# Up projections of a gated feed-forward with the product turned: high and low halves of the activations in one matmul

## The reference

```python
D_FF_2 = -(-8 * D_MODEL // (3 * 256)) * 256        # 2816

for l in range(DEPTH):                              # DEPTH = 2
    ...                                             # mixer, then cross attention
    h = rmsnorm(x, norm_ffn[l])                     # x: 256 x 1024
    x = x + (jax.nn.silu(h @ w1[l]) * (h @ w3[l])) @ w2[l]
```

## Time and profile before

| | before |
|---|---|
| median of 3 runs | 1738.66 us (1738.57 to 1738.78) |
| span of the profiled execution | 1736.9 us |
| TensorE busy | 1718.1 us (99%) |
| VectorE busy | 1123.0 us (65%) |
| ScalarE busy | 899.9 us (52%) |
| one steady group of it | 16.82 us |

### The profile page before, as it was taken

How to read it: one execution, slowest core, us unless ns; L and a number is a source line. 1 busy time by engine, 2 the same in 40 slices (tenths; PEclk the granted TensorE clock), 3 DMA queues, 4 the chain that set the end, 5 groups by cost and what they waited for, 6 DMA issues and landing times.

```text
span 1736.9 us, 23278 instructions
## 1 busy us (share of the span) xinstructions
PE 1718.1 (99%) x9541; PEld 1473.2 (85%) x9541; DVE 1123.0 (65%) x1324; ACT 899.9 (52%) x1048; POOL 170.5 (10%) x118
## 2 busy tenths in 40 slices
PE   8999999999999999999999999999999999999998
PEld 7888999888888888999888889888888888988886
DVE  6877655588677765655556686655555768665555
ACT  6665544465575555444455446544445544654443
POOL 2200000025253310000030000000003000000000
PEclk9999999999999999999999999999999999999999
DMA  8436555554535435555564564465546456446552
GB/s 287 172 137 216 185 182 189 194 165 154 189 119 183 162 122 197 192 195 194 170 216 149 204 226 149 131 209 189 180 165 207 157 201 218 146 156 196 193 189 78
DMA packets 160921, 311.10 MB, mean 179 GB/s; under 512 B 5723, under 2 KB 53344, under 8 KB 160048
## 3 DMA queue, kind: packets, MB, share of 16 engines
q1 hardware_dynamic: 158800, 299.33, 51.1%
q0 software_dynamic: 2016, 10.29, 1.7%
HBM read 304.35 MB, written 5.24 MB: 178 GB/s over the span
## 4 chain that ended last, share of the span: by engine, by line
PE 93%; DVE 4%; ACT 1%; issue 1%; DMA 1%; SPq 0%; DVEq 0%; ACTq 0%
PE ps L489 23%; PE ps L491 23%; PE ps L490 23%; PE ps L689 5%; PE ps L690 5%; PE ps L691 5%; PE ps L449 4%; DVE wlo L1549 1%; PE ps L623 1%; PE ps L647 1%; ACT whi L1001 1%; DVE nat L2086 1%; DMA raw<-in_a_w_qkv 1%; DVE hT_lo L1575 0%; DVE wide L2078 0%
## 5 line engine op out<-in xcount | busy, mean ns | idle before, releaser
L1549 DVE TENSOR_TENSOR wlo<-raw,whi 128x2048 fp32r<-128x2048 f32 x278 | 638.0, 2299 | 390.5 <-ACT whi L1001 390.1
L489 PE MATMUL ps<-whi,hT_hi 128*128 128x512 f32 (+1 forms) x1872 | 736.0, 393 | 3.0 <-DVE hT_lo L1575 0.8
L491 PE MATMUL ps<-whi,hT_lo 128*128 128x512 f32 (+1 forms) x1872 | 726.6, 388 | 0.0
L490 PE MATMUL ps<-wlo,hT_hi 128*128 128x512 f32 (+1 forms) x1872 | 725.7, 388 | 0.0
L1001 ACT ACTIVATE whi<-raw 128x2048 fp32r<-128x2048 f32 x278 | 531.8, 1914 | 349.6 <-PE ps L491 297.6
L489 PEld LDWEIGHTS ps<-whi,hT_hi 128*128 128x128 f32 x1872 | 351.8, 188 | 76.2 <-issue 6.6
L491 PEld LDWEIGHTS ps<-whi,hT_lo 128*128 128x128 f32 x1872 | 351.5, 188 | 73.1
L490 PEld LDWEIGHTS ps<-wlo,hT_hi 128*128 128x128 f32 x1872 | 352.0, 188 | 67.8
L689 PE MATMUL ps<-hT_hi,whi 128*128 128x256 f32 x768 | 218.7, 285 | 0.2
L691 PE MATMUL ps<-hT_hi,wlo 128*128 128x256 f32 x768 | 217.2, 283 | 0.0
L690 PE MATMUL ps<-hT_lo,whi 128*128 128x256 f32 x768 | 217.2, 283 | 0.0
(11 more groups left out here) (234 smaller groups left out, 1168.1 us busy)
## 6 DMA issues: line engine op xcount, KB each, us to landing
raw<-in_w_in SPq DMA_DIRECT2D x46, 1024.0 KB, 5.1
raw<-in_w SPq DMA_DIRECT2D x88, 512.0 KB, 4.5
raw<-in_m_w_up SPq DMA_DIRECT2D x32, 1024.0 KB, 5.2
raw<-in_m_w_down SPq DMA_DIRECT2D x32, 1024.0 KB, 4.9
raw<-in_kv_w SPq DMA_DIRECT2D x24, 1024.0 KB, 5.1
raw<-in_w SPq DMA_DIRECT2D x22, 1024.0 KB, 4.9
raw<-in_b_w_q SPq DMA_DIRECT2D x12, 1024.0 KB, 5.1
raw<-in_a_w_qkv SPq DMA_DIRECT2D x11, 1024.0 KB, 5.9
```

The source lines that it names most:

```text
L489: pe.matmul(acc, xh, wh, start=start and k == 0, stop=False)
L490: pe.matmul(acc, xh, wl, start=False, stop=False)
L491: ins = pe.matmul(acc, xl, wh, start=False, stop=stop and k == kc - 1)
L1549: vec.tensor_tensor(wlo[:, m % SPLIT, :], raw[:, m % RAW, :], whi[:, m % SPLIT, :], ALU.subtract).then_inc(*mark("lo_ready", ("lo", m)))
```

## The change

Only the up groups of the second block's feed-forward, and what follows them, are changed.

- The high and the low half of `hT[i]` become two halves of one buffer, `hT_both[i]`, so that one matmul can take a row block of both: 2 x 256 columns.
- `up_apart` takes the place of `chunk`. The weights are stationary, 128 columns at a time (4 blocks a tile: two of `w1`, two of `w3`), each block with a bank of its own. For each weight block and row block there is one matmul of 512 columns, `whi` by high and low tokens side by side, and one of 256, `wlo` by high tokens, added onto the first half of the bank. That is 2 x 4 x 4 x 2 = 64 matmuls a group. Four banks are used in place of two: `ACC`, `ACC + 1` and `OB`, `OB + 1` in group 0, `ACC`, `ACC + 1` and `TB`, `TB + 1` later.
- The product now has the tokens along the free axis, so r is needed as a row. VectorE writes r 128 times side by side (`r_wide`, L2227 of the changed kernel), TensorE turns that with two transposes after up group 0 (L999), ScalarE copies the row out (L1527).
- For each pair of banks ScalarE copies the low products out (L1533), VectorE adds them to the high ones (L2234) and multiplies by r (L2235). ScalarE makes the sigmoid (L1535), VectorE two products (L2237, L2238). ScalarE rounds the result into the high half of `hT[1]` (L1538), VectorE makes the low half (L2241). All of these are on 512 columns, as 2 x 256 where two banks are read.
- The gated chunk is not turned any more: `ff_turn`, its four transposes, and the copies L1018 and L1568 of it are gone. The down tile waits for `ff lo`.
- On VectorE the split that stood behind the gating of group 0 now stands ahead of it.

```diff
@@ TensorE
+            def up_apart(banks, turned=None, early=None):
+                ch = c.ch
+                hi, both = hT[0][0], hT_both[0]
+                for k0 in (0, 4):
+                    m = c.m
+                    pe.wait_ge(*at("lo", m))
+                    for nb in range(4):
+                        if k0 == 0 and (nb % 2 == 0 or early is not None and nb < 2):
+                            pe.wait_ge(*at("acc free", ch - 1, nb if early is not None and nb < 2 else nb // 2))
+                        for k in range(4):
...
+                            pe.matmul(ps[:, banks[nb], :], wh, both[:, :, k0 + k, :], start=k0 == k == 0, stop=False)
+                            ins = pe.matmul(ps[:, banks[nb], 0:S], wl, hi[:, k0 + k, :], start=False, stop=k0 == 4 and k == 3)
+                        if nb % 2:
+                            ins.then_inc(*mark("products", ("acc", m, nb // 2, 0)))
+                        if early is not None and k0 == 0 and nb == 1:
+                            early()
...
-                chunk(hT[0], tx[v + 2], early=lambda: x_half(v + 2, 1))
...
+                up_apart(UP_FIRST, tx[v + 2], lambda: x_half(v + 2, 1))
+                pe.wait_ge(*at("r wide", l))
+                for t in range(T):
+                    ins = pe.transpose(ps[:, SC, t * P:(t + 1) * P], r_wide[:, t, :], ident[:])
+                ins.then_inc(*mark("row_turned", ("r turned", l)))
                 for j in range(1, NG + 1):
                     if j < NG:
-                        chunk(hT[0], early=ff_turn if j == 1 else None)
-                    k0 = 2 * ((j - 1) % 2)
+                        up_apart(UP_LATER)
+                    pe.wait_ge(*at("ff lo", l, j - 1))
                     final = j == NG and l == L2 - 1
-                    tile(hT[1], k0, DN, j == 1, j == NG, tu[j - 1] - k0 // 2, None,
-                         ff_turn if j < NG else None if final else lambda: x_half(v + 3, 0), None, final)
+                    tile(hT[1], 2 * ((j - 1) % 2), DN, j == 1, j == NG, None, None,
+                         None if j < NG or final else lambda: x_half(v + 3, 0), None, final)
```

More of the change, by code:

```diff
@@ L702, in up_chunk @@
                         slot(n + k0 // 4)
+            def up_apart(banks, turned=None, early=None):
[8 more added lines that the diff above has]
+                        for k in range(4):
+                            if turned is not None and nb == 0 and k % 2 == 0:
+                                pe.wait_ge(*at("T free", turned + (k0 + k) // 2))
+                            w = k * 512 + nb * P
+                            wh, wl = whi[:, m % SPLIT, w:w + P], wlo[:, m % SPLIT, w:w + P]
+                            pe.matmul(ps[:, banks[nb], :], wh, both[:, :, k0 + k, :], start=k0 == k == 0, stop=False)
[4 more added lines that the diff above has]
+                            early()
+                    c.m += 1
+                c.ch += 1
             def mlp(v):
@@ L1500, in _ @@
                             begin(v + 2, junk2)
[L1501 to L1502 removed]
                         tick()
                         m = c.m - 1
[L1505 to L1511 removed]
+                        if j == 0:
+                            act.wait_ge(*at("r turned", l))
+                            sc.activation(r_row, ps[:, SC, 0:S], CP).then_inc(*mark("row_scales_turned", ("r row", l)))
+                        for b in range(2):
+                            act.wait_ge(*at("acc", m, b, 0))
+                            if j:
+                                act.wait_ge(*at("acc free", c.ch - 1, b))
+                            first = (UP_LATER if j else UP_FIRST)[2 * b]
+                            sc.activation(f_low[b], ps[:, first:first + 2, S:2 * S], CP).then_inc(*mark("low_products", ("ff low", l, j, b)))
+                        act.wait_ge(*at("ff scaled", l, j))
+                        sc.activation(f_s, f_a, ACT.Sigmoid).then_inc(*mark("sigmoids", ("fsig", l, j)))
+                        act.wait_ge(*at("ff", l, j))
+                        k = 2 * (j % 2)
+                        sc.activation(hT[1][0][:, k:k + 2, :], f_u, CP).then_inc(*mark("ff_hi", ("ff hi", l, j)))
                         c.ch += 1
@@ L2200, in _ @@
                             begin(v + 2)
[L2201 to L2204, removed]
+                            dve.wait_ge(*at("rs", v + 2))
+                            vec.tensor_copy(r_wide, bc(rst[:, o:o + T], 2, P)).then_inc(*mark("row_scales_wide", ("r wide", l)))
+                        tick()
                         if j == 0:
[L2206 to L2216, removed]
+                            dve.wait_ge(*at("r row", l))
+                        for b, f in enumerate((f_a, f_b)):
+                            first = (UP_LATER if j else UP_FIRST)[2 * b]
+                            dve.wait_ge(*at("ff low", l, j, b))
+                            settle(dve, vec.tensor_tensor(f, ps[:, first:first + 2, 0:S], f_low[b], ALU.add), "ff_sums", "acc free", c.ch, b)
+                            settle(dve, vec.tensor_tensor(f, f, bc(r_row, 1, 2), ALU.mult), "ff_scaled", "ff gain" if b else "ff scaled", l, j)
+                        dve.wait_ge(*at("fsig", l, j))
+                        settle(dve, vec.tensor_tensor(f_s, f_s, f_a, ALU.mult), "ff_steps", "ff1", l, j)
+                        settle(dve, vec.tensor_tensor(f_u, f_s, f_b, ALU.mult), "ff_ready", "ff", l, j)
+                        dve.wait_ge(*at("ff hi", l, j))
+                        hi, lo = [h[:, 2 * (j % 2):2 * (j % 2) + 2, :] for h in hT[1]]
+                        vec.tensor_tensor(lo, f_u, hi, ALU.subtract).then_inc(*mark("ff_lo", ("ff lo", l, j)))
                         c.ch += 1
@@ L2219, in _ @@
                         tick()
-                        turn(2, hT[1], None, 2 * (j % 2))
                 if l < L2 - 1:
```

18 lines of the change are left out of this document (6 added, 12 removed).

## The result

| | before | changed |
|---|---|---|
| median, 21 runs each | 1738.76 us | 1741.44 us |
| lowest to highest | 1738.45 to 1739.23 | 1740.47 to 1742.60 |
| span of the profiled execution | 1736.9 us | 1740.1 us |

The changed kernel is slower by 2.7 us; the ratio is 1.0015 with a 95% interval of 1.0009 to 1.0021, so within 0.2% or barely outside it. 3.1 us less were forecast. The time is just inside my upper end (1741.5), but the sign is wrong. And the executions of the changed kernel lie in two heaps: ten from 1740.47 to 1740.88, eleven from 1741.44 to 1742.60. Those of before lie within 0.8 us. The mean granted clock of an execution is 0.999 of full in all ten of the lower heap and 0.998 in ten of the eleven of the upper.

The account below looks back on a forecast made before the run. TensorE's slots were taken to bound the stage. Turns -11.0, up groups +4.7, wait at group 1 +3.3 and layer ends -0.1 gave -3.1 us: 1735.6 us from 1738.66, range 1730.8 to 1741.5.

Parts of the forecast that it names:

- What bounds the kernel, and the price of a slot: Changed stage: a string of TensorE slots, 226.7 ns per 512-column matmul and 119.9 per 256-column one, from first-block strings.
- The two equations: From first-block strings of 512 and 256 columns: 106.7 ns for 256 columns plus 13.3 ns for each matmul.
- The pair of alternating widths: Up groups: one wide and one narrow matmul together take 347 ns, adding 4.7 us over 22 groups.
- dear alternation: Up groups: split operand or wide slot staying 240 ns makes pairs 353 to 360 ns; 360 gives 1745.0 us; chance 0.14.
- The wait at group 1: Start of up group 1: TensorE waits for r's row and the low products, 1.64 us a layer, +3.3 us.
- The turns: Removed transposes of the gated chunk: 0.50 us of TensorE each, 22 of them, -11.0 us.
- Steady groups without waits: Steady up groups: chunk ready 5.1 us after a group's end, wanted at 16.5; no TensorE wait.
- S + 5.2: S is the end of an up group; the gated chunk was forecast ready 5.1 us after it.
- The ends: Layer ends, last down tile and turn of x: together 1.1 us saved, -0.1 us beyond the two turns counted.
- Columns alone: Rival, up groups: a narrow matmul after a wide one takes 113 ns, pairs 340; 1730.9 us; chance 0.16.
- late chain: Rival, steady groups: gating 3 us longer makes TensorE wait for the split in every group; 1741.6 us; chance 0.06.
- wait doubled: Rival, start of up group 1: the wait is twice the reckoned one; 1738.9 us, no change; chance 0.08.

## Why the prediction was wrong

- **What bounds the kernel, and the price of a slot: right.** The whole stage is slots. 226.7 ns for a wide one and 119.9 for a narrow one held wherever a string was long enough, the wide one also in the kernel with all matmuls wide. The two equations give 13.1 ns for each matmul, not 13.3, and nothing hangs on it. 13.4 ns is what remains of a wide slot over 512 columns at 2.4 GHz; the 2.5 ns that the Trainium skill gives ("TensorE: Matmul & The Clock Gate", "Wait — 56ns, not 53.3ns?") was not seen in any run here.
- **The pair of alternating widths: the step that failed.** I had seen both borders in the rows, 110 and 240 ns, and wrote that they "nearly cancel; I keep 347". Two digits of a timeline cannot carry that: 350 was what those rows gave, and I rounded it towards the string. A pair took 355, with what it does to the down tile's first slots, and 353 within the up group. The step mis-sized the term by 8 ns, which over the 18 steady groups alone is 4.7 us and turns the sign: +1.6 in place of -3.1. The rival "dear alternation" was the right one in its mechanism; its other half, the operand in two pieces, is refuted. I had put its break-even at 351.0 ns, so the profile of before left the sign open, and 0.14 for this rival was too little.
- **The wait at group 1: right in place, cause and size.** From the first transpose of r to group 1 it is 2.22 us, forecast 2.19. (That group 1 also starts at 1124.64, forecast 1124.7, is luck: group 0 began 0.25 us earlier and took 0.2 longer.) The second thing that the sum had at nothing: I did not see what a stand brings behind it: the half clock, 1.6 us each, in about half of the executions, +0.8 on the median. I had no rival for it; before, TensorE never stood long after its start, so its rows showed full clock; the longest distance between two starts in its trace is 1.45 us.
- **The turns: right,** 0.46 to 0.50 us each.
- **Steady groups without waits: right.** VectorE's part of a group ends at S + 5.2, forecast 5.1, and no wait of TensorE stands in 18 groups.
- **The ends: right.** The long slot at the last down tile is gone, and the turn of x in the first layer waits, for the reason given:

```profile
1297.88 0.39 PE L493 MATMUL ps<-whi,hT_both 128*128 128x512 f32 x1
1298.46 0.74 PE L451 MATMUL ps<-ident,x_res 128*128 128x128 f32 x5 [0.20 <-DVE x_res L1808]
```

0.58 between starts where a slot is 0.23: 0.35, with 0.5 expected.

- **Columns alone, late chain, wait doubled:** none came. The first pair behind a down tile does take 340 ns, but only the first.

## What to carry to other kernels

Where TensorE is the bound and two widths of matmul meet, measure or avoid their alternation; sorting the same matmuls into pairs or long strings of one width cost nothing and took 0.1 to 0.2 us off a group of 16.8. A rare wait of TensorE of 2 us and more deserves more care than its length says: look whether the granted clock falls behind it, and spread of the executions is the first sign of it. Where a row scaling comes late, free the banks with the sums first and scale afterwards.

## What the runs showed of the hardware

- A 512-column fp32r matmul takes 227 ns in a string and 233 to 241 behind a 256-column one in the steady groups; a pair of the two is 353 in the mean of an up group, 340 for the first behind a down tile. In one group, the same order took 347 a pair. Two and two take 348 a pair. The price is not a fixed one for each change of width; its rule is open.
- A moving operand in two pieces of 256 columns, 8 KB apart, is as cheap as one of 512.
- At ten of 16 traced stands of TensorE of 2.12 or 2.75 us between two starts, its granted clock was 0.5, that is 1.2 GHz, for a stretch of 3.4 us, which began between 0.3 us before the next matmul and 1.5 us after it. The same stand did it in one layer and not in the other of one execution. At stands of 1.99 us it was never seen, and transposes of the identity in the stand kept the clock up in the profiled execution.
